# A sixth raw slot for the first projection unit, and one map unit multiplied ahead of the transposes of x

## The reference, cut to what matters

```python
def _layer(x, cvec, p, kv_ctx):
    mod = jax.nn.silu(cvec) @ p['w_ada'] + p['b_ada']
    sh1, sc1, g1, sh2, sc2, g2 = [m[:, None, :] for m in jnp.split(mod, 6, axis=-1)]
    h = _rms_norm(x, p['norm1_g']) * (1 + sc1) + sh1
    mix, k, v = _mixing(h, p, kv_ctx)          # starts with h @ p['w_in']
    x = x + g1 * mix
    h2 = _rms_norm(x, p['norm2_g']) * (1 + sc2) + sh2
    x = x + g2 * _expert_choice_ffn(h2, p)     # 16 experts
    return x, k, v
```

## Time and profile before

| what | value |
|---|---|
| median of three runs | 1306.79 us (1306.72 to 1307.79) |
| the profiled execution, its own time | 1307.94 us |
| its span, first to last instruction | 1306.1 us |
| PE busy | 1215.0 us (93%) |
| DVE busy | 899.5 us (69%) |
| ACT busy | 617.0 us (47%) |
| mean rate of the DMAs over the span | 232 GB/s |
| mean granted clock of TensorE | 0.966 of full speed |

### The profile page before, as it was taken

One profiled execution on the slowest core, in us unless ns is written; L12 is line 12 of the kernel. 1 busy time (PEld: TensorE's weight loads), 2 busy tenths in 40 slices (PEclk: granted clock), 3 DMA queues, 4 the chain that ended last, 5 costly groups with the idle time before them and its releaser, 6 DMA issues.

```text
span 1306.1 us, 18927 instructions
## 1 busy us (share of the span) xinstructions
PE 1215.0 (93%) x7383; PEld 984.0 (75%) x7383; DVE 899.5 (69%) x1015; ACT 617.0 (47%) x686; POOL 311.3 (24%) x207
## 2 busy tenths in 40 slices
PE   4899879998999999999995399999999999999995
PEld 3798669998998999999995266666666666666663
DVE  3599766454553325523747489999999999999996
ACT  4311222224443124123213277777777777777774
POOL 1041100000443222323315202222222222222224
PEclk9899979999999989999997599999999999999998
DMA  9876642322111212244318999999999999999985
GB/s 321 266 205 208 200 93 65 100 78 73 50 50 65 65 33 65 80 162 146 100 44 314 333 346 368 381 379 380 380 379 380 381 381 381 380 381 381 386 312 179
DMA packets 156264, 302.89 MB, mean 232 GB/s; under 512 B 7058, under 2 KB 60821, under 8 KB 155952
## 3 DMA queue, kind: packets, MB, share of 16 engines
q1 hardware_dynamic: 145636, 272.80, 58.4%
q0 software_dynamic: 3872, 12.78, 4.3%
q10 hardware_dynamic: 6700, 16.51, 3.5%
HBM read 286.98 MB, written 15.08 MB: 231 GB/s over the span
## 4 chain that ended last, share of the span: by engine, by line
PE 86%; DVE 5%; DMA 3%; POOL 2%; ACT 1%; issue 1%; SPq 0%; ACTq 0%; POOLq 0%; DVEq 0%
PE bank L1500 17%; PE bank L1501 16%; PE bank L1502 16%; PE bank L1524 5%; PE bank L1526 5%; PE bank L1525 5%; PE bank L1528 5%; PE bank L1529 5%; PE bank L1527 5%; DMA wring<-in_w_ada 2%; PE bank L1752 2%; DVE fa L1060 1%; PE bank L1737 1%; PE bank L1805 1%; PE bank L1924 1%
## 5 line engine op out<-in xcount | busy, mean ns | idle before, releaser
L897 ACT CAST h2r_a<-w_a 128x2048 fp32r<-128x2048 f32 x96 | 183.7, 1914 | 84.8 <-PE bank L1502 77.0
L1500 PE MATMUL bank<-h2r_a,xTh 128*80 128x512 f32 x384 | 152.5, 397 | 1.0 <-DVE xTl L1417 1.0
L563 POOL TENSOR_TENSOR half<-half 1x1 f32<-1x1 f32 x33 | 69.7, 2112 | 351.3 <-DVE ye L1467 348.3
L1502 PE MATMUL bank<-h2r_a,xTl 128*80 128x512 f32 x384 | 150.5, 392 | 0.0
L493 POOL TENSOR_TENSOR lring<-wring,hring 128x2048 fp32r<-128x2048 f32 x21 | 99.1, 4719 | 178.5 <-ACT hring L631 178.5
L1501 PE MATMUL bank<-l2r_b,xTh 128*80 128x512 f32 x320 | 125.8, 393 | 0.0
L1411 DVE TENSOR_TENSOR l2r_b<-w_a,h2r_b 128x2048 fp32r<-128x2048 f32 x48 | 110.3, 2299 | 17.8 <-ACT h2r_b L897 17.8
L1411 DVE TENSOR_TENSOR l2r_b<-w_a,h2r_a 128x2048 fp32r<-128x2048 f32 x48 | 109.9, 2289 | 10.4 <-ACT h2r_a L897 10.4
L1411 DVE TENSOR_TENSOR l2r_a<-w_a,h2r_a 128x2048 fp32r<-128x2048 f32 x48 | 109.5, 2282 | 9.3 <-ACT h2r_a L897 7.7
L1060 DVE SCALAR_TENSOR_TENSOR fa<-fa,cwT 128x655 f32<-128x655 f32 x120 | 111.5, 972 | 1.4
L897 ACT CAST h2r_b<-w_a 128x2048 fp32r<-128x2048 f32 x48 | 91.9, 1914 | 34.7 <-PE bank L1502 31.9
(11 more groups left out here) (344 smaller groups left out, 3036.7 us busy)
## 6 DMA issues: line engine op xcount, KB each, us to landing
w_a<-in_w_e_gate SPq DMA_DIRECT2D x64, 1024.0 KB, 12.2
w_a<-in_w_e_up SPq DMA_DIRECT2D x64, 1024.0 KB, 13.0
w_b<-in_w_e_down SPq DMA_DIRECT2D x48, 1024.0 KB, 12.2
wring<-in_w_in SPq DMA_DIRECT2D x20, 1024.0 KB, 5.3
w_a<-in_w_e_down SPq DMA_DIRECT2D x16, 1024.0 KB, 13.1
fa<-in_w_ada SPq DMA_DIRECT2D x14, 1024.0 KB, 7.8
wring<-in_w_ada SPq DMA_DIRECT2D x10, 1024.0 KB, 9.2
fa<-in_w_in SPq DMA_DIRECT2D x4, 1024.0 KB, 11.2
```

The source lines that it names most:

```text
L897: act.copy(h2r[k % 3], w2[k]).then_inc(e_hi, 1)
L1500: pe.matmul(out, lh, rh, start=start, stop=False)
L1502: return pe.matmul(out, ll, rh, start=False, stop=stop)
```

## The change

In 0 gets a raw slot of its own, number 5, in a stretch of `fa` that nothing else uses then; its load has its own semaphore. Slot 3 then has ada 6 as its first unit. On PE, ada 2 and its turn 1 come ahead of the first transposes of x, and each later pair of transposes stands one map unit later: the order is ada 1, turn 0, ada 2, turn 1, x 0, x 1, ada 3, turn 2, x 2, x 3, ada 4, turn 3, x 4, x 5, ada 5, turn 4, x 6, x 7, and then the four steps of u2 block 0 as before. No instruction is added or removed. The orders of ACT, DVE, POOL and SP stay.

```diff
-        s_w = [sem(f"s_w{i}") for i in range(5)]
+        s_w = [sem(f"s_w{i}") for i in range(6)]
...
-        raw_slots = [wring[:, 0, :], wring[:, 1, :], fa[:, 8704:8704 + UN], fa[:, 6656:6656 + UN], fa[:, 2560:2560 + UN]]
+        raw_slots = [wring[:, 0, :], wring[:, 1, :], fa[:, 8704:8704 + UN], fa[:, 6656:6656 + UN], fa[:, 2560:2560 + UN], fa[:, 4608:4608 + UN]]
         SLOT = [u % 5 if u < FIVE else (u - FIVE + 2) % 4 if u < EARLY else u % 2 for u in range(N_U)]
+        SLOT[U_OF[("in", 0)]] = 5
...
-            for i in range(1, 6):
+            for i in (1, 2):
                 ada(i)
                 ada_turn(i - 1)
-                if i == 1:
-                    pe.wait_ge(s_xhat, TT)
-                if i < 5:
-                    turn_x(2 * i - 2)
-                    turn_x(2 * i - 1)
+            pe.wait_ge(s_xhat, TT)
+            for dc in range(DC):
+                turn_x(dc)
+                if dc % 2 == 1 and dc < 7:
+                    ada(3 + dc // 2)
+                    ada_turn(2 + dc // 2)
             first, u = in_block("u2", 0)
```

## The result

| kernel | median us (lowest to highest, executions) | ratio to before, 95% interval |
|---|---|---|
| before, beside it | 1306.10 (1304.88 to 1309.94, 11) | |
| after | 1309.92 (1307.61 to 1311.89, 11) | 1.0026 (1.0017 to 1.0035) |

The change made the kernel 0.26% slower, some 3.4 us. (The ratio is an estimate over all executions and not the quotient of the two medians, which differ by 3.8 us.) The profiled execution of after took 1309.75 us, its span is 1307.9 us, 1.8 us longer than that of before. That is less than the medians differ by, since the profile of before is of an execution 1.8 us above its median of 1306.10 us, and that of after is at its median within 0.2 us.

A forecast was written before the change was run, and what follows sets the result against it. The bound was TensorE's chain, with its long work starting at 49.7 us after the wait for ada 6's load. Slot -1.6 and order +1.5 gave 0.0 to +0.1 us: 1306.79 + 0.1 = 1306.9 us, range 1304.7 to 1309.7.

The forecast's parts named there:

- rival A: TensorE's clock stays low longer or falls at a new gap: +1.5 to +2.9 us, or near 1312; chance 0.28.
- the side that had 0.14: Whole kernel: a measurement that can be told from no change as slower, above 1309.4 us; chance 0.14.
- Part 1: Load of ada 6, with the slot of its own: ada 6 starts at 40.8 instead of 42.43, -1.6 us.
- the sum: Start of ada 6, both parts together: 42.3 to 42.5 against 42.43, 0.0 to +0.1 us.
- Part 2: PE's new order: x 3 ends 3.08 us later, passed through ACT and DVE to ada 6 as +1.5 us.
- The clock: TensorE's clock, the term least sized: by the skill's rule it rises no later; sum stays 0.0 to +0.1 us.
- the fall at 46 to 47: TensorE's clock before turn 7: falls behind two waits for loads; taken as staying, with no new one.
- Rival B: The clock's fall at 46 to 47 is spared: -2.1 us, 1304.7 us; chance 0.12.
- Rival C: Part 2's delay does not reach the four steps, Part 1 stands alone: -1.6 us, 1305.2 us; chance 0.06.
- Rival D: Ada 6's load is held up by something else, as SP's queue; result as the sum, joint chance 0.52.
- A gain up to 49.7 is a gain of the whole: PE's long dense work from 49.7 us on: nothing behind it has a start of its own.

The follow-up runs named there:

- e1: Against before: only the slot of its own for in 0, TensorE's order as before; 1307.68 us, ratio 1.0002.
- e12: Against before: the slot alone, plus idle transposes in all longer idle times of TensorE, also around ada 7; 1303.62 us, ratio 0.9969.
- e8: Against before: the slot alone, the very same kernel as e1, measured a second time; 1306.04 us, ratio 0.9991.
- e10: After with idle transposes in every longer idle time of TensorE up to the four steps; 1306.12 us, ratio to before 0.9996.
- e2: Against before: only TensorE's new order, with the old slots; 1311.13 us, ratio 1.0036.
- e6: After without the shift of the transpose pairs, so that only ada 2 and turn 1 are ahead; 1305.22 us, ratio to before 0.9987.
- e9: e6 with 22 idle transposes between turn 6 and turn 7; 1304.23 us, ratio to before 0.9974.
- e11: Before with idle transposes: 48 before ada 1, 12 behind turn 0, 10 behind x 3, 8 behind turn 4; 1307.23 us, ratio 1.0000.
- e3: After with 36 idle transposes early, in TensorE's idle time between 12.0 and 19.5; 1309.08 us, ratio to before 1.0020.
- e4: Before with the same 36 early idle transposes as e3; 1310.91 us, ratio 1.0031.

## Why the prediction was right or wrong

The forecast of 1306.9 us, no change, did not come; the ratio puts after at 1306.79 x 1.0026 = 1310.2 us (1309.0 to 1311.4), at and beyond the top of the range, 1309.7. On the median of all eleven executions of before, 1306.10, the same ratio gives 1309.5 us. What came is rival A, which had 0.28, and on the side that had 0.14.

- **Part 1, -1.6 us: near, and too large in the mean.** e1 shows 41.03 against 42.43, 1.4 us, and e12 the same. The term that was too small is the four steps: 3.5 us in the sum, some 3.8 in the rows (37.2 to 41.03 in e1). In the mean of two measurements the slot alone gave 0.5 us; a clock that rises late took the rest in the profile of e8, and how often is not shown. The prediction had laid that loss on the new order alone.
- **Part 2, +1.5 us: right at the full clock.** e10 follows it step by step. The losing step was ahead of it: ada 3 was put at 1.07 us, and x 2 and x 3 at the durations that x 4 and x 5 have in before, all of the full clock. In after x 1 ended at 27.56, near the "about 27" of the prediction, but x 3 at 33.6.
- **The clock: the step that failed**, "I take the fall at 46 to 47 as staying and no new one". The first half held, though the fall came only at 51 to 52 (0.83). No new fall is on record before it. What the sum left out is a late rise: it took the clock as up when ada 3 came, and ada 3, turn 2, x 2 and x 3 ran at the low level, which cost 2.4 us. That was not a rare case: the loss is in the median. The trace of before had the hint, and the prediction used it for the rival only: ada 1 and turn 0 raised nothing. The new order puts ada 2 and turn 1 behind them, more of the same, in place of transposes, and splits the transposes that follow.
- **Rival A's price**, x 3 later by 2.5 us "and the whole with it", was near: x 3 ended 2.4 us later than the sum has, and ada 6 started 2.3 us later. The kernel lost 3.4 us, while the two profiles differ by 1.8 us only; most of the rest is that the profile of before is itself 1.8 us above its median. Where that execution lost them is not shown. The rise in e2, within ada 5, shows that an execution can lose more at the start; whether those of after do was not seen, since each kernel has one profile. This part of the size stays open.
- **Rival B**, the spared fall, did not occur in after but was right as a mechanism: 2.1 us between the profiles of e6 and e9, 1.7 us between their ratios. Rival C is refuted by e10, where the delay of part 2 reaches the four steps, and ada 6, in full. Rival D is refuted by SP's rows.
- **A gain up to 49.7 is a gain of the whole**: it held for the part up to 160 us. Behind that the kernel's own clock falls again between 160 and 168 us, in every profile, for 7 to 17 us, and the length differs between executions (7 us in e11, 10 in e1 and e9, 17 in before and after). In e1 this gave 2.7 us more than the start had gained, in e2 it took back 1.5 of 4 us.

## What to carry to other kernels

Before moving small work on TensorE, look at which clock its rows have, and not only at the order of waits: a piece of dense work that seems off the critical path can be what brings the clock up for the pieces on it. Where TensorE must wait a few microseconds ahead of long work, transposes of a constant into an unused bank are a cheap way to hold the clock; they must not outlast the wait (0.46 us lost in e12), and one filled wait is not enough when the next ones stay open: in e3 and e4 the clock was up for ada 1 and fell behind the wait after it. A gain of 1.6 us in a start that the clock moves by 2 us from one execution to another needs medians over many executions, not one trace.

## What the runs showed of the hardware

- **When the clock came back.** The first instruction of mixed or full duration was turn 1 at 26.8 and ada 3 at 30.0 in two executions of the same kernel (e1, e8), ada 4 at 33.5 in after, ada 5 at 38.8 in e2, ada 2 at 24.9 in before. Each time two `turn_x` (ten records) or more stood in the stretch ahead of it, though two were not always enough: after had x 0 and x 1 at 25.2 to 27.6. In after and e6 PE worked through ada 1, turn 0, ada 2 and turn 1, from 19.5 and 19.8 on for over 5 us nearly without a gap, and all of them have the durations of the low level.
- **Transposes count.** The prediction quoted a rule of the Trainium skill (TensorE: Matmul & The Clock Gate, section Part 4: PE-mode transpose), that they don't count as work for the clock as matmuls do. By that rule the fillers could do nothing. For the fp32 transposes of this case the trace doesn't agree: within the 48 transposes of e10 the clock rose (7.23 us for 48, 0.15 each, where one takes 0.22 at the low level, as the five of x 0 in before, which took 1.12 us from the start of x 0 to that of x 1, and 0.12 at the full one, by 18 in 2.13 us). In e12 they took 7.92 us, behind only ada 0, an idle time of 2.9 us and five small transposes. With the further ones the clock of e10 stayed up to 50 us.
- **Gaps.** The clock fell behind gaps of 1.56 and 1.31 us with one map unit and one turn between them (e3), and behind gaps of 0.38 and 1.44 us with the same between them (e4). It fell again between 44 and 55 in all kernels that had no filler before turn 7: latest in e2 (window 54 to 55: 0.52), earliest in e4 (44 to 45: 0.80) and e11 (45 to 46: 0.56), whose ada 7 has it:

```profile
45.52 1.94 PE L1556 MATMUL bank<-fa 128*32 128x256 f32 x16 [1.39 <-DMA fa<-in_w_ada]
```

- **The clock column of a profile** says 1.00 from the start up to the first recorded change. After has 1.00 at 30 to 31 with ada 3 at 1.93 us, e3 has 0.50 there with 1.94 us. Up to the first fall, durations are the better witness.
